# Earlier loads of the cached keys and values, and a ring of three for the negated row minima, in the attention stage of a decoder layer

## The chip, the cores and the metric

The kernel runs on one core of a Trainium2 chip. The metric is the device time of one execution in microseconds. The engines are TensorE (matmuls), VectorE, ScalarE, GpSimd and SyncE; all but TensorE and VectorE issue DMAs here, and in the stage of this change all DMAs are issued by SyncE. In the profile they stand as PE (PEld for its weight loads), DVE, ACT, POOL and SP (SPq for what its queue issues).

## The reference

One layer of a decoder is computed for a prompt of 2048 tokens and for 8 samples of 4 new tokens each, whose past keys and values lie in a cache. The layer has a projection, a recurrent head group, dilated sliding-window attention, an output projection and a mixture of experts. The attention is what matters here:

```
DILATED_CONFIGS = ((128, 1), (512, 4), (2048, 16))      # window, dilation; 8 heads of 64

def _strided_band_attn(q, k, v, window, dilation):      # prompt: blocks of 128 rows of one residue
    ...
    sc = jnp.einsum('bnqhd,bnkhd->bnhqk', qb, kw).astype(jnp.float32) * dh ** -0.5
    sc = jnp.where(mask[None, :, None], sc, NEG_INF)
    m = jnp.max(sc, axis=-1, keepdims=True)
    p = jnp.exp(sc - m)
    l = jnp.sum(p, axis=-1, keepdims=True)
    o = jnp.einsum('bnhqk,bnkhd->bnqhd', (p / l).astype(v.dtype), vw)
    ...

def _dilated_attn_sample(q, k, v, k_buf, v_buf):        # samples: 129 keys per dilation, from the cache
    ...
        sc = jnp.einsum('bthd,btjhd->bthj', q, kg).astype(jnp.float32) * dh ** -0.5
        lse = jax.nn.logsumexp(sc, axis=-1)
        p = jnp.exp(sc - lse[..., None])
        outs.append(jnp.einsum('bthj,btjhd->bthd', p.astype(v.dtype), vg))
    ...
```

The results of the three dilations are merged with weights from their maxima and denominators; the kernel does that in a later stage, which reads what this stage stored.

## The kernel before, in words

The layer is a sequence of stages with a barrier between them. The change is in `attention` (from line 1224).

**Prompt.** There are 48 blocks of 128 query rows: 16 for each dilation. Each is worked in two halves of four heads, so there are 96 units u = 2n and 2n + 1. The first block of each residue has 128 keys, all others 256; the sixteen blocks of dilation 16 (n = 32 to 47) are all first blocks. Keys and queries lie in SBUF, transposed; the keys are turned block by block at the start (`turn_x`, line 1445). In round u of its loop TensorE computes the scores of unit u + 2 (line 1463), turns the probabilities of u (`turn_p`, line 1483), multiplies those of u - 1 with the values (`weigh`, lines 1497 and 1498), and in odd rounds does a piece of a sample's work. VectorE in round u first does the mask and the row minima of unit u + 2 (`mask_min`, line 1615; the queries carry the sign and the scale, so that the minimum of the negated score plays the part of the maximum), then copies half of the turned probabilities (`p_copy`, line 1623), then does a piece of a sample's work. ScalarE takes the exponentials of u + 1 (line 1565) with the minima as bias, copies the other half, and copies the result of u - 1 to the tile `O`, a ring of NO = 3 (line 1579), for which it waits until the stores of block n - 3 have landed.

**Minima.** They are written to `NM`, one tile for all 48 blocks, and nobody waits to write there. The result tile and the minima of block n are stored by `store(n)` (lines 1306 and 1307), both counted by the semaphore `o_st[n % NO]`.

**Samples.** Sample b has a place in the loop, `at(b) = 13 + 8 * b`. Its cached keys come in three groups (256 KiB, 1 MiB and 1 MiB, for dilations 1, 4 and 16), its cached values likewise, its query as a broadcast to all partitions (1 MiB), and its new value rows as 8 KiB. GpSimd multiplies keys by query (`product`, line 1414); the product of the third group, and so on, waits for VectorE's sum of the product two before it, as these are double buffered. VectorE sums (line 1646) in rounds at(b) - 6, - 5 and - 3; in round at(b) the scores are turned and their maxima taken, in round at(b) + 4 the probabilities are turned back, GpSimd spreads them by key tile (line 1422), and in round at(b) + 6 TensorE multiplies them by the cached values in 18 matmuls (`weigh_sample`, line 1518).

**The queue.** SyncE issues every DMA of this stage in one order, written out by hand. In iteration n it issues the key block n + 3 (line 1290, while there are any), the prompt values of block n + 2 (line 1300), then what the samples need (lines 1311, 1317, 1329, 1335 and 1336), and last the store of block n - 1, before which it waits until both halves of that block have been copied. So it enters iteration n once block n - 2 is stored. Each load of a buffer still in use waits first, in the queue's order: `load_sample_k(b, g)` for the product of sample b - 1 and group g, `load_sample_v(b, g)` for the last matmul of sample b - 1, `store_sample(b)` for its result.

By iteration, the samples' DMAs were placed like this, with b counted so that all are for sample b:

| DMA | before | after |
|---|---|---|
| keys, first group | 1 + 4b | 4b - 1 |
| query, keys second group | 2 + 4b | 4b - 1 |
| keys, third group | 3 + 4b | 4b + 1 |
| values, first and second group | 8 + 4b | 7 + 4b |
| values, third group, and new value rows | 9 + 4b | 7 + 4b |
| stores of its result (six) | 12 + 4b | 11 + 4b |

Sample 0 is loaded at n = 0 to 4 in both, and its keys and values are left out of the table; in the kernel before the stores of sample 7 stand at n = 40, in the kernel after at n = 39.

## Time and profile before

| | |
|---|---|
| median of 3 runs | 3607.88 us (3606.35 to 3614.04) |
| the profiled execution | 3606.35 us |
| its span, first to last instruction | 3604.6 us |
| TensorE matmul, share of the span | 88% |
| VectorE, ScalarE, GpSimd | 37%, 28%, 9% |
| HBM read and written | 409.18 MB and 148.50 MB |
| attention stage | about 1612 to 2067 us |
| its work on VectorE at the mask, line 1615 | 384 instructions, 117.3 us |

The span is what the profiler saw from the first instruction to the last; the execution's own time has 1.8 us more around it. A matmul's busy time overlaps the next one's. In rows of a timeline the columns are start, duration, engine, line, operation, output and input tile, and in brackets the idle time of the engine before it with what ended it. In rows of stretches they are the stretch and its length, then busy time and instructions of each engine, the granted TensorE clock (1.00 is 2.4 GHz, 0.50 is 1.2 GHz), the share of time in which the 16 DMA engines were busy, and GB/s.

### The profile page before, as it was taken

To read this page: it belongs to the slowest core of one execution; us is meant where nothing else is said; L and a number is where in the kernel's file an instruction comes from. 1 tells how busy PE (TensorE), PEld (TensorE's weight loads), DVE (VectorE), ACT (ScalarE), POOL (GpSimd) and SP (SyncE) were. 2 spreads that over 40 slices of the span, in tenths; PEclk is the share of its full clock that TensorE was granted. 3 is DMA by queue.
4 is the path that set the end of the run, shared out by engine and by line. 5 is a ranking of instruction groups with operands and counts; after the bars stand their busy time and mean duration, and the time that the engine had idled before them with its cause. 6 is when DMAs were issued, how large, how long until landed. Compare 5 with 4: busy or idle time off the path is not lost. (4 is left out here: it accounts for less than half of the span.)

```text
span 3604.6 us, 75447 instructions
## 1 busy us (share of the span) xinstructions
PE 3171.0 (88%) x31053; PEld 2166.8 (60%) x31054; DVE 1331.3 (37%) x3298; ACT 1013.7 (28%) x2152; POOL 319.3 (9%) x343
## 2 busy tenths in 40 slices
PE   6999999999879888969999859986999999999920
PEld 4667766667668888867776725543555555555500
DVE  3445544444134333426655346643111111111135
ACT  4334443333222222216444523320111111111112
POOL 0000000000010000003432000000001110111011
PEclk9999999999679999989999979987999999999965
DMA  6111111111542323328555465515778776676755
GB/s 216 49 66 65 65 49 60 55 51 56 66 169 109 110 101 115 120 91 266 185 177 154 105 224 177 168 59 206 251 244 279 247 275 221 245 278 211 249 195 204
DMA packets 302886, 561.48 MB, mean 156 GB/s; under 512 B 98866, under 2 KB 123186, under 8 KB 295972
## 3 DMA queue, kind: packets, MB, share of 16 engines
q1 hardware_dynamic: 267684, 458.90, 38.1%
q0 software_dynamic: 20784, 73.15, 5.5%
q10 hardware_dynamic: 14160, 25.70, 2.1%
q8 instruction: 198, 3.24, 0.4%
q14 instruction: 60, 0.49, 0.0%
HBM read 409.18 MB, written 148.50 MB: 155 GB/s over the span
## 5 line engine op out<-in xcount | busy, mean ns | idle before, releaser
L294 PE MATMUL proj_main_ps<-proj_xt,proj_w 128*128 128x257 f32 (+1 forms) x1728 | 391.4, 382 | 0.0
L294 PEld LDWEIGHTS proj_main_ps<-proj_xt,proj_w 128*128 128x128 f32 x1728 | 329.5, 204 | 40.9
L2409 PE MATMUL moe_gate<-moe_w,moe_xt 128*64 128x256 f32 x2624 | 299.7, 382 | 6.6 <-DMA moe_w<-in_expert_w_dram 5.9
L2425 PE MATMUL moe_y_ps<-moe_w,moe_ht 128*64 128x512 f32 x1312 | 301.2, 601 | 3.1 <-ACT moe_ht L2464 3.1
L2409 PE MATMUL moe_up<-moe_w,moe_xt 128*64 128x256 f32 x2624 | 301.3, 383 | 0.0
L2409 PEld LDWEIGHTS moe_gate<-moe_w,moe_xt 128*64 128x64 f32 x2624 | 189.6, 138 | 136.9 <-issue 47.8
L317 PE MATMUL proj_main_ps<-proj_w,proj_xt 128*128 128x512 f32 (+1 forms) x560 | 249.1, 599 | 0.0
L2162 PE MATMUL out_proj_ps<-out_w,out_ct 128*128 128x512 f32 x544 | 240.6, 596 | 0.0
L2409 PEld LDWEIGHTS moe_up<-moe_w,moe_xt 128*64 128x64 f32 x2624 | 180.3, 137 | 97.4 <-issue 13.6
L2475 ACT ACTIVATE moe_sg<-moe_gate 128x256 f32<-128x256 f32 x82 | 31.4, 383 | 542.0 <-PE moe_gate L2409 542.0
L2425 PEld LDWEIGHTS moe_y_ps<-moe_w,moe_ht 128*64 128x64 f32 x1312 | 87.3, 137 | 158.6 <-issue 155.2
L1148 DVE COPY_PREDICATED rwkv_t<-rwkv_cons,rwkv_level_ps 128x512 f32<-128x512 uint32 (+1 forms) x168 | 109.3, 660 | 188.8 <-PE rwkv_level_ps L866 188.7
L317 PEld LDWEIGHTS proj_main_ps<-proj_w,proj_xt 128*128 128x128 f32 (+1 forms) x560 | 103.1, 185 | 124.5 <-issue 123.0
L2511 DVE COPY moe_y<-moe_y_ps 128x512 f32<-128x512 f32 x82 | 56.7, 692 | 313.6 <-PE moe_y_ps L2425 313.6
L2162 PEld LDWEIGHTS out_proj_ps<-out_w,out_ct 128*128 128x128 f32 x544 | 101.7, 192 | 115.1 <-issue 115.1
L1615 DVE CUSTOM_DVE_ANT_0 att_sc<-att_s_ps,att_mask 128x256 f32<-128x256 f32 (+1 forms) x384 | 117.3, 361 | 106.0 <-PE att_s_ps L1463 105.9
L866 PE MATMUL rwkv_level_ps<-rwkv_t,rwkv_w 64*64 64x64 f32 x2688 | 152.5, 222 | 3.4 <-issue 3.4
L2460 ACT COPY moe_xt<-moe_xt_ps 128x512 f32<-128x512 f32 x83 | 48.6, 585 | 353.7 <-PE moe_xt_ps L2402 353.7
L1565 ACT ACTIVATE att_sc<-att_sc,att_nm 128x256 f32<-128x256 f32 (+1 forms) x384 | 145.5, 453 | 0.0
L2517 DVE TENSOR_TENSOR moe_hd<-moe_sg,moe_gate 128x256 f32<-128x256 f32 x82 | 34.6, 421 | 286.4 <-ACT moe_sg L2475 286.4
L1463 PE MATMUL att_s_ps<-att_kt,att_qt 64*128 64x256 f32 (+1 forms) x768 | 139.3, 490 | 0.9 <-DVE att_pt L1623 0.5
L866 PEld LDWEIGHTS rwkv_level_ps<-rwkv_t,rwkv_w 64*64 64x64 f32 x2688 | 135.2, 138 | 4.9 <-issue 4.9
(336 smaller groups left out, 5093.7 us busy)
## 6 DMA issues: line engine op xcount, KB each, us to landing
moe_w<-in_expert_w_dram SPq DMA_DIRECT2D x96, 2048.0 KB, 10.3
y_rows<-rwkv_zero POOLq DMA_DIRECT2D x65, 512.0 KB, 4.8
y_rows<-moe_y ACTq DMA_DIRECT2D x164, 128.0 KB, 6.2
ft_p<-proj_uf SPq DMA_DIRECT2D x32, 642.0 KB, 3.4
rwkv_feat<-ft_p SPq DMA_DIRECT2D x16, 1284.0 KB, 7.2
att_s_k<-in_cache_att_k_dram SPq DMA_DIRECT2D x16, 1024.0 KB, 8.1
att_s_v<-in_cache_att_v_dram SPq DMA_DIRECT2D x16, 1024.0 KB
o_p<-att_o SPq DMA_DIRECT2D x48, 260.0 KB, 2.1
```

Of the source, the lines that this page charges most:

```text
L294: last = mm(out[:, 0:w + 1], W[:, k, kind * C + m * P:kind * C + (m + 1) * P], XT[n % 2][:, k, 0:w + 1], start=(k == 0), stop=(k == KT - 1))
L317: last = mm(o, x, W[:, k, j * C:(j + 1) * C], start=(k == 0), stop=(k == KT - 1))
L866: last = mm(level_ps[g][part(c), hh * P + DH:(hh + 1) * P], W[g][part(c), hh, :], T[i % 3][part(c), h, DH:P], start=True, stop=True, skip_ ...
L1148: v.copy_predicated(T[i % 3][:, 4 * g:4 * g + 4, k0:P], wide(level(l)[:, k0:P], 4).bitcast(U32), four(level_ps[g][:])[:, :, k0:P]).then_in ...
L1463: last = mm(s_ps[u % 2][e][:, pl * 2 * P + k_from(u):(pl + 1) * 2 * P], QT[rows, q, q_at:q_at + d * (P - 1) + 1:d], KT[rows, q, k_at:k_at ...
L1565: nc.scalar.activation(SC[u % NSC][:, hl, k0:], SC[u % NSC][:, hl, k0:], ACT.Exp, bias=NM[:, n, 4 * half + hl:4 * half + hl + 1], scale=-1 ...
L1615: v.tensor_tensor_reduce(SC[u % NSC][:, hl, k0:], s_ps[u % 2][e][:, pl * 2 * P + k0:(pl + 1) * 2 * P], mask[:, k0:], 1.0, 3e38, ALU.add, A ...
L2162: last = mm(proj_ps[j][:], CT[t % 2][:, k, :], W[:, k, 512 * j:512 * (j + 1)], start=(k == 0), stop=(k == KT - 1))
L2409: last = mm(bank[j * HB:(j + 1) * HB, 0:HF], XT[:, q, r * HB:(r + 1) * HB], W[:, k, j * HF:(j + 1) * HF], start=(k == 0), stop=(k == KT - ...
L2425: last = mm(py[j * HB:(j + 1) * HB, :], HT[:, c, r * HB:(r + 1) * HB], W2[s][:, k, j * 512:(j + 1) * 512], start=(k == 0), stop=(k == FE / ...
L2460: nc.scalar.copy(XT[:].rearrange("p k t -> p (k t)"), px[:]).then_inc(xt_ready, 1)
L2511: v.tensor_copy(Y[:], py[:]).then_inc(y_ev, 1)
```

## The change

The minima go into a ring of three small tiles instead of one large one. Because a tile is used again three blocks later, VectorE waits, ahead of the first half of block n, until the stores of block n - 3 have landed. The samples' values are loaded in one place instead of two; keys, queries, values and the samples' stores are issued in earlier iterations of SyncE's loop, as the table above shows. Of the loads of sample b + 1 the query and the first two groups of keys now stand in iteration 3 + 4b, which is also the iteration in which the values of sample b - 1 and the stores of sample b - 2 stand.

```diff
--- before.py
+++ after.py
@@ -1244,7 +1244,7 @@
         V = ring("v", [P, H, VW], NV)
         SC = ring("sc", [P, 4, 2 * P], NSC)
         PT = ring("pt", [P, 4, 2, P], 2)
-        NM = sb("nm", [P, NBK, H])
+        NM = ring("nm", [P, H], NO)
         O = ring("o", [P, H, VW], NO)
         s_ps = [[ps(f"s_ps{k}_{e}") for e in range(2)] for k in range(2)]
         t_ps = [ps(f"t_ps{j}") for j in range(2)]
@@ -1304,7 +1304,7 @@
                 sp.wait_ge(o_copied, 2 * n + 2)
                 dst = lambda x: x[c].rearrange("(i d) k -> d i k", d=d)[r, b * P:(b + 1) * P, :]
                 sp.dma_start(dst(o_out), O[n % NO][:].rearrange("p h k -> p (h k)")).then_inc(o_st[n % NO], 16)
-                sp.dma_start(dst(m_out), NM[:, n, :]).then_inc(o_st[n % NO], 16)
+                sp.dma_start(dst(m_out), NM[n % NO][:]).then_inc(o_st[n % NO], 16)
 
             def load_sample_q(b):
                 rows = qkv_s[b * T:(b + 1) * T, 0:C]
@@ -1321,12 +1321,12 @@
                     sp.wait_ge(s_prod, 3 * (b - 1) + g + 1)
                 cached(SK, cache_k, b, g, sk_ld[g])
 
-            def load_sample_v(b, g):
+            def load_sample_v(b):
                 if b >= 1:
                     sp.wait_ge(s_weighted, b)
-                cached(SV, cache_v, b, g, sv_ld)
-                if g == 2:
-                    sp.dma_start(VN[:], qkv_s[b * T:(b + 1) * T, 2 * C:3 * C]).then_inc(sv_ld, 16)
+                for g in range(3):
+                    cached(SV, cache_v, b, g, sv_ld)
+                sp.dma_start(VN[:], qkv_s[b * T:(b + 1) * T, 2 * C:3 * C]).then_inc(sv_ld, 16)
 
             def store_sample(b):
                 sp.wait_ge(s_o, b + 1)
@@ -1362,28 +1362,20 @@
                 if 1 <= n < 3:
                     load_sample_k(0, n)
                 if n == 4:
-                    for g in range(3):
-                        load_sample_v(0, g)
-                for b in range(B + 1):
-                    slot = n - (at(b) - 7) // 2
-                    if slot == 1 and b >= 2:
-                        load_sample_v(b - 1, 0)
-                        load_sample_v(b - 1, 1)
-                        store_sample(b - 2)
-                    if slot == 2 and b >= 2:
-                        load_sample_v(b - 1, 2)
-                    if b + 1 < B:
-                        if slot == 2:
-                            load_sample_k(b + 1, 0)
-                        if slot == 3:
-                            if b >= 1:
-                                sp.wait_ge(s_prod, 3 * b)
-                            load_sample_q(b + 1)
-                            load_sample_k(b + 1, 1)
-                        if slot == 4:
-                            load_sample_k(b + 1, 2)
-                if n == (at(B - 1) + 11) // 2:
-                    store_sample(B - 1)
+                    load_sample_v(0)
+                for b in range(B):
+                    if n == (at(b) - 7) // 2 and b + 1 < B:
+                        if b >= 1:
+                            sp.wait_ge(s_prod, 3 * b)
+                        load_sample_q(b + 1)
+                        load_sample_k(b + 1, 0)
+                        load_sample_k(b + 1, 1)
+                    if n == (at(b) - 3) // 2 and b + 1 < B:
+                        load_sample_k(b + 1, 2)
+                    if n == (at(b) + 9) // 2:
+                        if b + 1 < B:
+                            load_sample_v(b + 1)
+                        store_sample(b)
                 if n >= 1:
                     store(n - 1)
             store(NBK - 1)
@@ -1562,7 +1554,7 @@
                 k0 = k_from(u)
                 for hl in range(4):
                     a.wait_ge(masked, 4 * u + hl + 1)
-                    nc.scalar.activation(SC[u % NSC][:, hl, k0:], SC[u % NSC][:, hl, k0:], ACT.Exp, bias=NM[:, n, 4 * half + hl:4 * half + hl + 1], scale=-1.0).then_inc(exped, 1)
+                    nc.scalar.activation(SC[u % NSC][:, hl, k0:], SC[u % NSC][:, hl, k0:], ACT.Exp, bias=NM[n % NO][:, 4 * half + hl:4 * half + hl + 1], scale=-1.0).then_inc(exped, 1)
 
             def p_copy(u):
                 a.wait_ge(p_turned, u + 1)
@@ -1610,10 +1602,12 @@
                 v.wait_ge(scored, u + 1)
                 if u >= NSC:
                     v.wait_ge(p_turned, u - NSC + 1)
+                if n >= NO and half == 0:
+                    v.wait_ge(o_st[n % NO], 32 * (n // NO))
                 for hl in range(4):
                     pl, e = hl // 2, hl % 2
                     v.tensor_tensor_reduce(SC[u % NSC][:, hl, k0:], s_ps[u % 2][e][:, pl * 2 * P + k0:(pl + 1) * 2 * P], mask[:, k0:], 1.0, 3e38,
-                                           ALU.add, ALU.min, NM[:, n, 4 * half + hl:4 * half + hl + 1]).then_inc(masked, 1)
+                                           ALU.add, ALU.min, NM[n % NO][:, 4 * half + hl:4 * half + hl + 1]).then_inc(masked, 1)
 
             def p_copy(u):
                 v.wait_ge(p_turned, u + 1)
```

## Rows read from the trace of the kernel before

**Rows 1.** The page: the engines over the whole span.

```profile
PE 3171.0 (88%) x31053; PEld 2166.8 (60%) x31054; DVE 1331.3 (37%) x3298; ACT 1013.7 (28%) x2152; POOL 319.3 (9%) x343
```

**Rows 2.** Busy time by stretch, attention stage.

```profile
1700.00:1750.00 50.00, 49.94 (x357) 38.24 (x356) 33.37 (x101) 28.52 (x68) 16.50 (x5) 1.00 0.67 198
```

**Rows 3.** Waits, attention stage: who for whom, total us, times, longest.

```profile
DVE att_sc L1615 <- PE att_s_ps L1463: 105.9, 71, 17.9
...
PE att_t_ps L1518 <- issue: 8.8, 2, 4.6
```

**Rows 4.** Timeline of TensorE: the value products of samples 1, 6 and 7.

```profile
1747.96 7.92 PE L1518 MATMUL att_t_ps<-att_s_v,att_s_lm 128*96 128x512 f32 x18
...
1967.12 9.76 PE L1518 MATMUL att_t_ps<-att_s_v,att_s_lm 128*96 128x512 f32 x18 [4.20 <-issue]
...
2003.86 10.16 PE L1518 MATMUL att_t_ps<-att_s_v,att_s_lm 128*96 128x512 f32 x18 [4.60 <-issue]
```

**Rows 5.** Timeline of SyncE's queue at the last samples, and two stretches.

```profile
1956.63 0.59 SPq L1317 DMA_DIRECT2D att_s_v<-in_cache_att_v_dram  x1
...
1957.00:1961.00 4.00, 4.00 (x32) 3.47 (x33) 2.76 (x13) 2.54 (x9) 2.27 (x2) 1.00 0.46 34
1961.00:1967.00 6.00, 1.93 (x18) 1.58 (x16) 2.61 (x10) 2.85 (x10) 0.00 (x0) 0.75 0.96 283
```

**Rows 6.** Timeline of SyncE's queue, iterations 11, 15 and 19.

```profile
1719.51 0.32 SPq L1306 DMA_DIRECT2D o_p<-att_o  x1
...
1720.35 1.14 SPq L1290 DMA_DIRECT2D att_x<-out_dram  x1
...
1727.95 0.33 SPq L1306 DMA_DIRECT2D o_p<-att_o  x1
...
1761.16 0.33 SPq L1306 DMA_DIRECT2D o_p<-att_o  x1
...
1805.85 0.33 SPq L1306 DMA_DIRECT2D o_p<-att_o  x1
```

**Rows 7.** Timeline of VectorE and TensorE, masks of blocks 13, 17, 21.

```profile
1733.25 0.41 DVE L1615 CUSTOM_DVE_ANT_0 att_sc<-att_s_ps,att_mask 128x256 f32<-128x256 f32 x1
...
1735.44 0.61 PE L1445 MATMUL att_t_ps<-att_ident,att_x 128*128 128x128 f32 x4
...
1774.80 0.42 DVE L1615 CUSTOM_DVE_ANT_0 att_sc<-att_s_ps,att_mask 128x256 f32<-128x256 f32 x1 [0.98 <-PE att_s_ps L1463]
...
1779.24 0.42 DVE L1615 CUSTOM_DVE_ANT_0 att_sc<-att_s_ps,att_mask 128x256 f32<-128x256 f32 x1 [0.45 <-PE att_s_ps L1463]
...
1781.10 0.30 PE L1511 MATMUL att_t_ps<-att_ident,att_s_p 96*128 96x96 f32 x1 [0.47 <-DVE att_pt L1623]
...
1820.55 0.42 DVE L1615 CUSTOM_DVE_ANT_0 att_sc<-att_s_ps,att_mask 128x256 f32<-128x256 f32 x1 [0.98 <-PE att_s_ps L1463]
```

**Rows 8.** By line: key load 1639.2, minima's store 1644.3, all their stores.

```profile
L1317 SPq DMA_DIRECT2D att_s_k<-in_cache_att_k_dram x1: 1902/1902/1902, 1639.2 to 1639.2; - x1
...
DMA to landing us min/median/max: 10.1/10.1/10.1
...
L1307 SPq DMA_DIRECT2D m_p<-att_nm x1: 433/433/433, 1644.3 to 1644.3; - x1
...
DMA to landing us min/median/max: 5.8/5.8/5.8
...
DMA to landing us min/median/max: 1.9/1.9/6.3
```

**Rows 9.** SyncE's queue (packets, MB, share), 1719 to 1762; one stretch.

```profile
q1 hardware_dynamic: 7289, 8.46, 65.1%
...
1658.00:1666.00 8.00, 7.38 (x65) 6.57 (x63) 6.91 (x20) 4.31 (x10) 4.54 (x1) 1.00 1.04 376
```

**Rows 10.** Timeline of GpSimd.

```profile
1649.44 4.54 POOL L1414 TENSOR_TENSOR att_s_prd<-att_s_k,att_s_q 128x2048 f32<-128x2048 f32 x1 [10.53 <-DVE att_s_sn L1630]
...
1752.74 9.01 POOL L1414 TENSOR_TENSOR att_s_prd<-att_s_k,att_s_q 128x2048 f32<-128x2048 f32 x2 [10.15 <-DMA att_s_q<-qkv_s]
```

## The prediction

> **What bounds the kernel now.** I read the page first for the share of each engine [rows 1], then TensorE's stretches in the attention stage, the only stage that the change touches [rows 2]. The stage runs from about 1612 to 2067 us, a little over an eighth of the span. From 1700 to 1750 us TensorE is busy 49.94 of 50 us, so a microsecond that TensorE loses there is a microsecond of the kernel. I then read the waits of the stage [rows 3]. No row there makes TensorE, VectorE or ScalarE wait for a load of cached keys. VectorE's waits at the mask (line 1615) are waits for TensorE, 105.9 us in 71 pieces: it has slack on average, and the question is how much of it lies at the places where the change adds a wait. Two waits are not slack. The product of probabilities and cached values (line 1518) is preceded by 8.8 us of idle TensorE in two pieces.
>
> The timeline shows them [rows 4]: before the seventh and the eighth sample TensorE idles 4.20 and 4.60 us, and its 18 matmuls then take 9.76 and 10.16 us where an undisturbed sample's take 7.92 us. The queue explains it [rows 5]: the last 1 MiB of the seventh sample's values is issued at 1956.63, moves only from about 1961 us on (34 GB/s from 1957 to 1961, 283 GB/s from 1961 to 1967), and TensorE starts at 1967.12. The granted clock was 0.75 on average from 1961 to 1967, so in part of it the level of 1.2 GHz, and TensorE had just gone idle.
>
> **Earlier values: a gain.** Values move from iterations n = 8 and 9 + 4b of SyncE's loop to 7 + 4b, for all but the first sample. For the eighth sample that is two iterations of some 6 us before the old last part. Both stalls should go: 4.20 + 4.60 + (9.76 - 7.92) + (10.16 - 7.92) = 12.9 us. From below the gain is nothing, if the stall has another cause. No other sample waits (two pieces in all), so earlier values are worth nothing there.
>
> **Where the loads now meet.** In the new loop, iterations n = 11, 15, 19, 23 and 27 issue, all ahead of the store of block n - 1: a prompt value block (256 KiB), all values of a sample (2.25 MiB), its new value rows, six small stores of the previous sample, a query broadcast (1 MiB) and two groups of keys (1.25 MiB). With the 260 KiB store behind them this is 5.26 MB, where one iteration had 2.25 MiB at most in steady state. SyncE alone needs about 8 us to issue it (16 DMAs, and those in rows 6 take 0.3 to 1.1 us each), as much as a block lasts (1719.5 to 1728.0).
>
> **The new wait.** The mask minima go into a ring of three, so the mask of block m + 3 (VectorE) now waits for the stores of block m. Call T the time at which block n - 2 is stored. The store of block n - 1 comes about 8 to 9 us after T, and the mask that needs its landing started at 1733.25 for n = 11, which is T + 13.7, and at 1774.80 for n = 15, T + 13.6 [rows 6, 7]. For n = 19 (T = 1805.85) it started at 1820.55, T + 14.7; I use that for 23 and 27. The store leaves at 1727.95 for n = 11 and such a store lands 1.9 us after its issue in the median [rows 8], so in the old rhythm it is there some 3 us ahead, and the wait alone costs nothing: what covers it is TensorE's own unit of work between the two.
>
> Behind the burst it doesn't. A store issued at 1644.30 while a 1 MiB key load from 1639.2 was still on its way (it took 10.1 us, to 1649.3) took 5.8 us, to 1650.1 [rows 8]. I read this as one queue served in order. The first load leaves at T + 0.85 (1720.35 - 1719.51). The rate: over a period of four blocks the queue moved 8.46 MB in 65.1% of 43 us, 302 GB/s while it moved, and the best long stretch has 376 GB/s [rows 9]. I take 320, nearer to the first, which has the same mix of transfers. So 5.26 MB take 16.4 us; with the 1.9 us that a small store takes alone the store lands at T + 0.85 + 16.4 + 1.9 = T + 19.2. For n = 11, with one more 256 KiB block of keys ahead, it lands at 1720.35 + 17.3 + 1.9 = 1739.5.
>
> How much lateness VectorE can take is in rows 7. At n = 11 the copy behind the mask ends just where TensorE turns the next key block (1735.44), so none. At n = 15 it works on from the first mask to the second with 0.45 us of idle ahead of that (1779.24), and TensorE already waits 0.47 us for the copy after it (1781.10): 0.45 us can be absorbed. The next ones have the same pattern. Stalls of TensorE: n = 11: 1739.5 - 1733.25 = 6.3; n = 15: 19.2 - 13.6 - 0.45 = 5.1; n = 19, 23, 27: 19.2 - 14.7 - 0.45 = 4.05 each, 12.15. Sum 23.5 us. Lower bound with 376 GB/s: 3.7 + 2.65 + 3 x 1.6 = 11 us. Upper bound with 302 GB/s and the 3.5 us in which the queue moved nearly nothing after the last part of the values was issued [rows 5]: 10.8 + 9.6 + 3 x 8.5 = 46 us.
>
> The Trainium skill (DMA: Bandwidth & Descriptors, section Where 436 GB/s comes from) puts the limit of one core's HBM traffic at about 358 GB/s; the trace has 376 over 8 us, so the measurement decides. By an estimate from that page the five stalls would add up to about 15 us instead of 23.5.
>
> **Clock.** An idle of 4.20 us cost another 1.84 us through matmuls at half clock [rows 4]. The five stalls are of that length, so 5 x 1.84 = 9.2 us; from below nothing, if shorter gaps leave the clock alone, and 5 x 2.24 = 11 us from above.
>
> **Start.** At n = 3 the second sample's second key group waits for the product of the first sample's second group, which ends at 1649.44 + 4.54 = 1654.0 [rows 10], and store 2 stands behind it, then the values of the first sample at n = 4. Queries and keys of 1.25 MiB also enter a queue that at 1649.3 had only just landed the key load before them and still held the last 1 MiB of the prompt's queries [rows 8]. From 1649.3 some 3.6 MB at 320 GB/s put the landing near 1661, while store 2 is due 8.4 us after the one of 1644.3 and its landing needed 5.3 us later (1733.25 - 1727.95), at 1658. I take 3.5 us, between 1 and 10. **Tail.** At n = 35 values, prompt values and six small stores (2.89 MB) precede store 34: it lands at T + 11.8, needed at about T + 9 because these blocks last 5.2 us, with about 1 us of slack: 1.5 us, between 0 and 5. At n = 7 (2.75 MiB of loads) and 31 the store lands within a microsecond of its need: 0.
>
> **Costed at nothing.** The ring's smaller tile and its other addresses. ScalarE's wait for the same store comes later than VectorE's and is met. The old loads' removal from n = 5 to 9: nobody waited. GpSimd's products move earlier (in rows 10 they wait 10.15 us for a query), with VectorE's sums where they were. SyncE's waits on products in steady state: even at their old place the products ended at 1752.74 + 9.01 = 1761.75, before SyncE asks, after 1762 [rows 6, 10].
>
> **Sum.** 23.5 + 9.2 + 3.5 + 1.5 - 12.9 = +24.8 us. The profiled execution took 3606.35 us (span 3604.6, 1.8 us around it), so 3631.2; the median of the runs is 1.5 us above it: 3632.7, and I say 3633.
>
> **Rivals.** *Stalls gone, none new (faster).* The store isn't held up, or VectorE's slack covers it, and only the 12.9 us are seen: 3595. For it: the old queue was drained when a store came, and VectorE idles 106 us at this line. Against it: it needs 5.26 MB within 11 us, 480 GB/s, or a store that overtakes, which rows 8 contradict. It decides if the store lands before T + 13.7. Chance 0.13.
>
> *Even.* The queue runs at its best rate and the gaps are too short for the clock: 11 + 1 - 12.9 = about 0, 3607. Chance 0.13 for all within 0.2% (7.2 us, about what a measurement of this kernel can tell).
>
> *SyncE held at a product.* The third load of the burst waits for GpSimd; if products ended 3 us later than before, each of five bursts would grow by 3 us: 3648. Against it: their queries now come earlier. Chance 0.04.
>
> *Values are not why TensorE idles.* Then 12.9 us stay lost: 3646. Against it: the stretches of rows 5, where data move until TensorE starts. Counted with the next case. *Queue much slower.* All upper bounds: 46 + 11 + 10 + 5 - 12.9 = +59, 3667. Together 0.06. My forecast, slower by 8 to 54 us, has 0.64.
>
> **Range.** The low end is the even case with part of the faster one, 3603, and the high end 3662; beyond lie 0.12 and 0.06. Slower by over 0.2%: 0.64 + 0.04 + 0.06 = 0.74.
>
> **What the profile after would show.** VectorE's idle before line 1615 released by a store of the minima, in about five pieces of 4 to 6 us plus a few short ones. Landings of the two block stores near 10 us at n = 11 to 27, and SyncE issue times of several us at the query or key loads. TensorE idle in the same places, with clock 0.5 behind. No idle before line 1518 at the seventh and eighth samples. It is wrong if the stores land in 2 us behind the loads, if the burst drains at over 450 GB/s, or if VectorE had more slack than I read.

## The result, and the profile after

The kernel after takes 3694.68 us (median of 4 runs, 3690.24 to 3702.20), the kernel before, run beside it, 3610.96 us. The ratio is 1.0232, with a 95% interval of 1.0207 to 1.0259: slower by 84 us. The prediction had the sign, and 25 us. The profiled execution took 3683.05 us with a span of 3681.3, 76.7 us more than the one of before. Between these two executions the rest of the program, which the change leaves as it was, took 9.6 us less (7.6 ahead of the attention stage, 2.0 behind it), and the stage itself 86.3 us more. The stretches of the stage, from its first matmul to its last, in the kernel before and in the kernel after:

```profile
1616.05:2066.02 449.97, 431.36 (x2817) 327.61 (x2817) 252.17 (x963) 230.62 (x608) 129.41 (x33) 0.97 0.59 181
```

```profile
1608.48:2144.79 536.31, 478.84 (x2817) 371.03 (x2817) 249.87 (x963) 231.95 (x608) 129.26 (x33) 0.82 0.52 151
```

With the same 2817 matmuls TensorE is idle for 38.9 us more (57.5 against 18.6) and busy for 47.5 us more, at a granted clock of 0.82 on average instead of 0.97. All sums below are made against these 86.3.

The waits of the attention stage in the kernel after (who for whom, total us, times, longest), which answer to [rows 3]:

```profile
DVE att_sc L1609 <- DMA m_p<-att_nm: 68.0, 11, 11.6
...
ACT att_sc L1557 <- DVE att_nm L1609: 28.1, 8, 7.0
PE att_t_ps L1475 <- DVE att_pt L1617: 19.4, 4, 6.8
```

The first row is new: VectorE, at the mask, waits eleven times for a store of the minima. The others are its followers: ScalarE's exponentials wait for the minima, TensorE for VectorE's copies. The row of 8.8 us of idle before the value product, the second of [rows 3], has no successor: these waits are gone.

TensorE's timeline shows where this costs time (start, duration, instruction, idle before it and what ended it). These are six of the fourteen gaps over 1 us behind the start of the stage; together the fourteen make 51.1 us.

```profile
1658.91 1.09 PE L1437 MATMUL att_t_ps<-att_ident,att_x 128*128 128x128 f32 x4 [4.96 <-issue]
...
1748.55 1.09 PE L1437 MATMUL att_t_ps<-att_ident,att_x 128*128 128x128 f32 x4 [11.45 <-issue]
1801.25 1.09 PE L1475 MATMUL att_t_ps<-att_ident,att_sc 128*128 128x128 f32 x4 [6.82 <-DVE att_pt L1617]
...
2014.25 0.30 PE L1503 MATMUL att_t_ps<-att_ident,att_s_p 96*128 96x96 f32 x1 [1.81 <-DVE att_pt L1617]
2053.68 1.09 PE L1475 MATMUL att_t_ps<-att_ident,att_sc 128*128 128x128 f32 x4 [6.25 <-ACT att_sc L1557]
2090.28 0.63 PE L1475 MATMUL att_t_ps<-att_ident,att_sc 128*128 128x128 f32 x4 [1.64 <-ACT att_sc L1557]
```

The burst of iteration n = 11 in SyncE's queue, the same iteration as the first two rows of [rows 6]: block 9 is stored at T = 1721.00, and the minima's store of block 10 is issued behind all loads of the burst.

```profile
1721.00 0.32 SPq L1306 DMA_DIRECT2D o_p<-att_o  x1
...
1729.91 1.02 SPq L1317 DMA_DIRECT2D att_s_k<-in_cache_att_k_dram  x2
1730.97 0.48 SPq L1306 DMA_DIRECT2D o_p<-att_o  x1
1731.51 0.49 SPq L1307 DMA_DIRECT2D m_p<-att_nm  x1
```

By line, that store of the minima, and below it the same for one store in the last blocks:

```profile
L1307 SPq DMA_DIRECT2D m_p<-att_nm x1: 491/491/491, 1731.5 to 1731.5; - x1
...
DMA to landing us min/median/max: 14.7/14.7/14.7
...
L1307 SPq DMA_DIRECT2D m_p<-att_nm x1: 433/433/433, 2083.1 to 2083.1; - x1
...
DMA to landing us min/median/max: 5.6/5.6/5.6
```

And VectorE's masks that waited, in bursts 11 and 15, and in the last blocks:

```profile
1746.37 0.43 DVE L1609 CUSTOM_DVE_ANT_0 att_sc<-att_s_ps,att_mask 128x256 f32<-128x256 f32 x1 [11.55 <-DMA m_p<-att_nm]
...
1799.30 0.42 DVE L1609 CUSTOM_DVE_ANT_0 att_sc<-att_s_ps,att_mask 128x256 f32<-128x256 f32 x1 [10.25 <-DMA m_p<-att_nm]
...
2052.26 0.29 DVE L1609 CUSTOM_DVE_ANT_0 att_sc<-att_s_ps,att_mask 128x128 f32<-128x128 f32 x1 [8.70 <-DMA m_p<-att_nm]
2088.86 0.29 DVE L1609 CUSTOM_DVE_ANT_0 att_sc<-att_s_ps,att_mask 128x128 f32<-128x128 f32 x1 [4.08 <-DMA m_p<-att_nm]
```

SyncE issues the burst in about 10 us and is held by nothing in it (the longest issue takes 1.60 us); the queue does the rest. The store issued at 1731.51 lands 14.7 us later, at 1746.2, and the mask starts at once: at T + 25.4, where before it started at T + 13.7 [rows 7]. In the next two bursts (T = 1776.39 and 1830.79) the mask starts at T + 22.9 and T + 22.0.

The last reading is of the clock (stretch, then busy time and instructions by engine, the granted clock, the DMA share, GB/s):

```profile
1740.00:1750.00 10.00, 1.46 (x6) 1.16 (x8) 3.63 (x10) 0.33 (x1) 0.00 (x0) 0.50 1.01 336
1750.00:1760.00 10.00, 10.00 (x75) 8.42 (x75) 6.83 (x22) 5.81 (x14) 4.21 (x2) 0.85 0.04 16
...
2090.00:2100.00 10.00, 9.72 (x54) 8.95 (x54) 4.08 (x28) 4.69 (x15) 0.00 (x0) 0.55 0.31 81
...
2130.00:2140.00 10.00, 10.00 (x54) 9.32 (x53) 3.14 (x19) 5.63 (x18) 0.00 (x0) 0.50 0.08 29
```

In the middle the 10 us behind the longest gap average 0.85. In the last blocks, after a gap of 1.64 us, it is at 0.50 until the stage ends, although TensorE is counted busy for 10.00 of 10 us. But the clock also falls where no gap stands ahead. Call a sample's value product (18 matmuls of 512 columns) dense, and the blocks' own matmuls, of 64 to 256 columns, light. At 1879.3, 1933.9 and 1988.6 the clock falls about 3 us behind the end of a dense product, with TensorE busy throughout, and the first time it is back at 1889.6, in the middle of light blocks:

```profile
1880.00:1889.00 9.00, 9.00 (x43) 7.93 (x41) 3.57 (x17) 2.87 (x7) 0.00 (x0) 0.50 0.29 79
1890.00:1900.00 10.00, 10.00 (x77) 9.07 (x78) 6.07 (x23) 6.07 (x18) 0.00 (x0) 1.00 1.06 301
```

What the lower clock costs in the last blocks is seen in the timeline: one unit of those blocks in the kernel after,

```profile
2103.74 1.24 PE L1455 MATMUL att_s_ps<-att_kt,att_qt 64*128 64x128 f32 x8
2104.91 1.11 PE L1475 MATMUL att_t_ps<-att_ident,att_sc 128*128 128x128 f32 x4
2105.82 1.80 PE L1490 MATMUL att_o_ps<-att_v,att_pt 128*128 128x65 f32 x8
2107.55 1.24 PE L1455 MATMUL att_s_ps<-att_kt,att_qt 64*128 64x128 f32 x8
```

and one at a granted clock of 1.00, in the run e13 told below, which has the same queue:

```profile
2067.88 1.23 PE L1455 MATMUL att_s_ps<-att_kt,att_qt 64*128 64x128 f32 x8
2069.04 0.66 PE L1475 MATMUL att_t_ps<-att_ident,att_sc 128*128 128x128 f32 x4
2069.53 1.00 PE L1490 MATMUL att_o_ps<-att_v,att_pt 128*128 128x65 f32 x8
2070.48 1.23 PE L1455 MATMUL att_s_ps<-att_kt,att_qt 64*128 64x128 f32 x8
```

A unit lasts 3.81 us (1.24 to 1.24) instead of 2.60. From 2090.9 to the last product, which ends at 2144.8, are 14.1 such units: 14.1 x 1.21 = 17 us.

**The ledger of the 86.3 us.** Idle that is new: 51.1 us, of it 35.3 in the five bursts, 6.1 at the start, 1.8 at n = 31 and 7.9 in the last blocks. Idle that is gone: 8.8 before the value products and 3.5 in small pieces and in the stage's first microseconds. Together that is 38.9, up to rounding. The 47.5 us in which TensorE is busy for longer with the same matmuls I put down to the lower clock: 17 of it in the last blocks by the rows above, and some 30 elsewhere, net of what the two old gaps had cost. These 30 are a difference and are not split further; part of them is in the three stretches (24 us in all) that no gap precedes.

### The profile page after: what moved, and what is told of

Its sections match the earlier page's. It is cut to its first block and busy times, and to the rows that moved or that the text cites. A ratio compares the mean times of both kernels' runs of the same rounds, so it can differ in the third digit from the quotient of the medians.

```text
span 3681.3 us, 75447 instructions
## 1 busy us (share of the span) xinstructions
PE 3211.8 (87%) x31053; PEld 2202.3 (60%) x31054; DVE 1328.4 (36%) x3298; ACT 1014.6 (28%) x2152; POOL 319.6 (9%) x343
## 5 line engine op out<-in xcount | busy, mean ns | idle before, releaser
L1490 PE MATMUL att_o_ps<-att_v,att_pt 128*128 128x65 f32 x768 | 149.4, 314 | 0.0
```

The source lines that it names most:

```text
L1490: last = mm(out, PT[u % 2][:, hl, 1, :], V[n % NV][:, h, :], start=first(u), stop=True, skip_group_check=True)
```

## The experiments

Fourteen kernels ran. Each ratio is to runs of the kernel before beside it, on the same chip (medians 3592.95 for e1 to e4, 3586.83 for e5 to e8, 3592.18 for e9 to e12, 3591.45 for e13 and e14).

**The parts by themselves.** e1 is the kernel before with the ring and the wait alone:

```
-        NM = sb("nm", [P, NBK, H])
+        NM = ring("nm", [P, H], NO)
...
+                if n >= NO and half == 0:
+                    v.wait_ge(o_st[n % NO], 32 * (n // NO))
```

> The kernel before with the ring of three for the minima and its wait, and the old order of SyncE's queue. Theory (the wait costs only where a burst of loads stands ahead of the store): VectorE's waits for a store of the minima come to a few us in all, most of them at the start, and the time is 3611 to 3622 us; a single late landing among the last blocks may add up to 20 us through the clock. Rival (the ring alone is the cost): 3670 us or more, with waits in nearly every period of four blocks.

e2 is the kernel after with one tile of minima and no wait, so the new queue alone:

```
-        NM = ring("nm", [P, H], NO)
+        NM = sb("nm", [P, NBK, H])
...
-                if n >= NO and half == 0:
-                    v.wait_ge(o_st[n % NO], 32 * (n // NO))
```

> The changed kernel with one tile for all minima and no wait on VectorE; its queue as changed. Theory: the stores still land 15 to 25 us late behind the bursts, but nobody needs them then, so the only effect left is the one of the early values, -12.9 us: 3598 us, up to 3608 if ScalarE's wait for the same stores, three rounds later, now binds by a few us. Rival (the loads themselves do the harm, through late prompt values or contention): over 3630 us.

e3 is the kernel before with only the values read together and an iteration earlier:

```
+                    if slot == 0 and b >= 2:
+                        for g in range(3):
+                            load_sample_v(b - 1, g)
                     if slot == 1 and b >= 2:
-                        load_sample_v(b - 1, 0)
-                        load_sample_v(b - 1, 1)
...
-                        load_sample_v(b - 1, 2)
```

> The kernel before with one tile for all minima, and of the change only this: the values of samples 1 to 7 issued together in iteration 7 + 4b. Theory: TensorE no longer idles before the value products of the seventh and eighth samples (4.2 and 4.6 us) and its clock doesn't fall there: 3598 us, between 3594 and 3604. Rival (the stall there has another cause): 3611 us.

e4 is the kernel after with a ring of six, so that a block waits for stores six blocks back:

```
-        NM = ring("nm", [P, H], NO)
+        NM = ring("nm", [P, H], 2 * NO)
...
+                if n >= 2 * NO and half == 0:
+                    v.wait_ge(o_st[n % NO], 32 * (n // NO - 1))
```

> The changed kernel with a ring of six tiles for the minima, so that VectorE waits for the stores of block n - 6, some 25 us further back. Theory (the depth of the ring is what fails against bursts of about 20 us): no wait for a store of the minima over 1 us, and the time of the kernel with one tile and the new queue, 3598 to 3608 us. Rival (the wait itself, as an instruction, costs): between 3620 and 3690 us.

Measured: e1 3611.96 us, ratio 1.0056 (1.0038 to 1.0074); e2 3589.58 us, 0.9985 (0.9970 to 1.0000); e3 3594.53 us, 0.9999 (0.9978 to 1.0020); e4 3587.33 us, 0.9991 (0.9972 to 1.0010). The ring alone costs 20 us, the queue alone costs nothing, and both together 84: most of the loss comes only with both. With a ring of six VectorE waits for no store, and the loss is gone. The wait of e1 is short in the middle, where the old queue holds no burst, but it is not free. The row of its waits, and its longest, in VectorE's timeline:

```profile
DVE att_sc L1617 <- DMA m_p<-att_nm: 23.9, 8, 6.8
```

```profile
1995.24 0.29 DVE L1617 CUSTOM_DVE_ANT_0 att_sc<-att_s_ps,att_mask 128x128 f32<-128x128 f32 x1 [6.76 <-DMA m_p<-att_nm]
```

Five of its eight waits are in the last blocks, which last 5.2 us each. (This profile is of the fastest of its six runs, so it shows less than the 20 us.) The prediction had costed the wait alone at nothing. In e3 the idle before the value products is gone and the time is not: the stretch

```profile
2020.00:2060.00 40.00, 40.00 (x212) 36.36 (x210) 14.90 (x99) 20.33 (x64) 0.00 (x0) 0.50 0.24 68
```

of its profiled execution shows the last blocks at the lower clock with no gap of TensorE ahead of them: it fell at 1996.0, 3 us behind the eighth sample's dense product, and stayed for 68 us. So these blocks can lose their clock without the wait too, in some executions. The same happens in the middle: in e4, where VectorE waits for no store, light blocks run for 34 us at half clock behind a dense product, and in e2 for 28 us, until the next one.

```profile
1790.00:1824.00 34.00, 34.00 (x158) 29.99 (x157) 14.86 (x53) 12.24 (x32) 4.56 (x1) 0.50 0.62 182
```

**What makes the store late.** e5 puts keys and queries back where they were, so that a burst is split:

```
-                        load_sample_q(b + 1)
-                        load_sample_k(b + 1, 0)
-                        load_sample_k(b + 1, 1)
...
+                        if slot == 2:
+                            load_sample_k(b + 1, 0)
+                        if slot == 3:
...
+                            load_sample_q(b + 1)
+                            load_sample_k(b + 1, 1)
```

> The changed kernel with the ring of three and its wait, and with the values and the result stores where the change put them, but with queries and keys at the places of the kernel before. The burst ahead of store n - 1 falls from 5.26 MB to about 3.9 MB where the third key group stands in it too, and the query is gone. Theory (the landing is late by what stands ahead of it): the waits at n = 11 to 27 shrink by about 5 us each, from 7 to 11.5 us to 2 to 6 us, and the time is 3615 to 3640 us against 3593 of before on that chip. Rival (any burst of values holds the store as long, because of a pause in the queue and not of bytes): over 3655 us.

e6 lets ScalarE's queue issue the blocks' stores, behind its second copy of the result, in place of SyncE's:

```
+                if half == 1:
...
+                    a.dma_start(dst(o_out), O[n % NO][:].rearrange("p h k -> p (h k)")).then_inc(o_st[n % NO], 16)
+                    a.dma_start(dst(m_out), NM[n % NO][:]).then_inc(o_st[n % NO], 16)
```

> The changed kernel with the two stores of each block issued by ScalarE after its copy, so that they don't stand behind the loads in SyncE's queue; loads and ring as changed. Theory (one queue served in order holds the stores): they land in 2 to 5 us even beside a burst, VectorE waits for minima's stores under 10 us in all instead of 68, and the time is 3595 to 3615 us, with some us for 0.8 us of issue per block on ScalarE. Rival (the memory or the DMA engines themselves are full, whatever the queue): waits of over 5 us in each burst and over 3640 us.

e7 moves the six small stores of a sample's result behind the block's stores:

```
-                        store_sample(b)
                 if n >= 1:
                     store(n - 1)
+                for b in range(B):
+                    if n == (at(b) + 9) // 2:
+                        store_sample(b)
```

> The changed kernel with only the six small result stores of a sample moved behind the block's stores in the same iteration. They are 25 KB in rows of 4 and 260 bytes. If they cause the pause of about 4 us that the queue shows inside each burst, the waits of VectorE shrink by 3 to 4 us each, and the time by 20 to 30 us, to 3645 to 3655 us where the changed kernel would take about 3677 on that chip. If the bytes ahead are what counts, the waits stay as they are and the time within 10 us of the changed kernel's.

Measured: e5 3640.33 us, 1.0157 (1.0130 to 1.0184), waits 41.2 us in 9; e6 3666.12 us, 1.0215 (1.0188 to 1.0241); e7 3673.91 us, 1.0242 (1.0215 to 1.0269), waits 57.5 us in 10. Splitting the burst takes a third of the loss away: the waits in the five bursts fall to 2.6 to 6.1 us, as expected, but 56 us over the kernel before beside it is more than the theory's 22 to 47; a wait of 8.4 us stays among the last blocks. In e7 the time is after's, as expected if the bytes ahead are what counts; what it says of the small stores is told below. e6 is the miss that teaches most. Its minima's store in the burst of n = 11, issued at 1730.70, lands in two thirds of the time. Its waits:

```profile
DVE att_sc L1612 <- DMA m_p<-att_nm: 64.5, 17, 7.1
```

That store by line:

```profile
L1574 ACTq DMA_DIRECT2D m_p<-att_nm x1: 472/472/472, 1730.7 to 1730.7; - x1
...
DMA to landing us min/median/max: 9.4/9.4/9.4
```

The long waits shrink to 4.4 to 7.1 us, but seventeen waits add up to as much as eleven did, so "one queue served in order" was only part of the reason: a 4 KB store takes 9.4 us beside 5 MB of loads from another queue as well, where only the 260 KB store of the same block stands ahead of it. The Trainium skill (DMA: Bandwidth & Descriptors, section Issuing engines are not separate DMA queues) says that DMAs of all issuers run on the same 16 engines and interleave; the run agrees, with these 9.4 us. Another issuer shares the delay out instead of removing it.

**What the rate in a burst is.** In each burst the queue has a weak stretch of about 4 us (1735 to 1739 in the first, at T + 14):

```profile
1735.00:1737.00 2.00, 2.00 (x20) 1.95 (x18) 0.00 (x0) 0.87 (x2) 2.00 (x1) 1.00 0.91 156
1737.00:1739.00 2.00, 0.09 (x1) 0.00 (x0) 0.00 (x0) 0.38 (x1) 2.00 (x1) 1.00 0.83 90
...
1741.00:1743.00 2.00, 0.00 (x0) 0.00 (x0) 0.00 (x0) 0.00 (x0) 0.00 (x0) 0.50 0.98 395
```

The DMA engines are counted busy at 0.83 to 0.91 in it and move 90 to 156 GB/s. e10 takes a suspect out, the 8 KB load of the new value rows:

```
-                sp.dma_start(VN[:], qkv_s[b * T:(b + 1) * T, 2 * C:3 * C]).then_inc(sv_ld, 16)
+                if b == 0:
+                    sp.dma_start(VN[:], qkv_s[b * T:(b + 1) * T, 2 * C:3 * C]).then_inc(sv_ld, 16)
...
-                pe.wait_ge(sv_ld, 64 * b + 64)
+                pe.wait_ge(sv_ld, 48 * b + 64)
```

> The kernel after, without the 8 KB transfer of the new value rows of samples 1 to 7 (they use sample 0's, so that part of the computation is left out). Theory (this small transfer is what makes the weak stretch of about 4 us in each burst): the waits for the minima's buffer in blocks 11, 15, 19, 23 and 27 shrink by 3 to 4 us each, the time falls by 10 to 20 us. Rival (the weak stretch belongs to the large transfers themselves, or to their order): waits and time as after, within 5 us.

Measured: 3670.58 us, 1.0224 (1.0180 to 1.0268), waits 58.4 us in 9, longest 10.4. That is after's loss: the rival. So it isn't the value rows. The six small stores are not cleared by e7. There they are issued 4 us later, counted from T, land within 13 us of their issue, and the weak stretch comes later too, at T + 20 to T + 26 (T = 1718.59), still ahead of the landing of block 10's minima at T + 23.6:

```profile
1739.00:1741.00 2.00, 0.00 (x0) 0.00 (x0) 0.00 (x0) 0.00 (x0) 0.00 (x0) 0.50 1.22 130
1741.00:1743.00 2.00, 0.00 (x0) 0.00 (x0) 0.59 (x3) 0.00 (x0) 0.00 (x0) 0.50 0.94 134
```

The last blocks say the same. In the kernel after the six small stores of sample 7, at n = 39, stand right ahead of block 38's, which lands after 5.6 us, and block 41 waits. In e7 they stand one store further back: block 39's then takes 6.1 us, and the wait is at block 42. In e1 they are at n = 40, again ahead of block 39's, which takes 5.1 us, and again block 42 waits. The wait moves with them, so they make that one. For the weak stretch it is only where it lies that points to them; no run leaves them out of a burst, so its cause is not shown.

**What a gap costs, and where.** e8 and e9 hold VectorE up by the same work in the kernel before, in round 78 (last blocks) and in round 24 (middle):

```
+            def hold():
+                for j in range(4):
+                    v.wait_ge(q_ld[j], 16)
+                for j in range(2):
+                    v.tensor_reduce(IDLE[:, j * 8:(j + 1) * 8], QT[:, j, :].rearrange("p (h k) -> p h k", h=8), AX.X, ALU.add)
...
+                if u == 78:
+                    hold()
```

> The kernel before with one added delay of about 4.4 us on VectorE (two sums over 2048 columns of the queries, results unused) ahead of the mask in round 78, among the last blocks. Theory (a gap there takes the clock of TensorE to its lower level, and nothing in this light work brings it back before the stage ends): 2 to 3 us of idle, then granted clock 0.50 until the end of the stage, blocks of 7.64 instead of 5.19 us, in all 15 to 25 us more than before. Rival (the clock comes back after some us, as it did in the middle of the stage before): 4 to 6 us more.

> The kernel before, with VectorE held up by some 4.4 us once more, now in round 24, in the middle of the kernel, where a sample's dense attention product follows within 25 us (the earlier hold was in the last blocks). The work that holds it is two added sums, whose results nothing uses. Theory (a gap costs its own idle, and the clock is given back soon where dense work follows; in the last blocks it isn't): TensorE idle 2 to 4.5 us, 1 to 3 us more at the lower clock, 4 to 7 us in all, against 25 us for the same hold in the last blocks. Rival (a gap costs the same anywhere, the 25 us came from something else in the added sums): 20 us or more here too. Second rival (TensorE's queue of work covers it): under 2 us.

Measured: e8 3615.47 us, 1.0071 (1.0045 to 1.0097); e9 3596.09 us, 1.0019 (0.9997 to 1.0042). The same hold costs 25 us (16 to 35) in the last blocks and 7 (-1 to 15) in the middle, although TensorE's gap is the shorter one there. e8's gap, 1.83 us, in TensorE's timeline, and the stretches behind it:

```profile
2023.12 0.69 PE L1484 MATMUL att_t_ps<-att_ident,att_sc 128*128 128x128 f32 x4 [1.83 <-ACT att_sc L1566]
```

```profile
2020.00:2030.00 10.00, 8.17 (x49) 7.40 (x48) 5.59 (x28) 4.67 (x15) 0.00 (x0) 0.68 0.21 56
2030.00:2040.00 10.00, 10.00 (x54) 9.09 (x53) 4.07 (x27) 5.04 (x16) 0.00 (x0) 0.50 0.33 93
```

The stretches of e9, with its gap of 4.19 us in the first of them (the last row begins within the second):

```profile
1720.00:1730.00 10.00, 5.81 (x42) 4.88 (x43) 10.00 (x13) 3.38 (x8) 4.52 (x1) 0.80 0.62 196
1730.00:1740.00 10.00, 10.00 (x76) 8.46 (x74) 6.88 (x22) 5.87 (x15) 2.02 (x1) 0.86 0.39 142
1733.00:1743.00 10.00, 10.00 (x88) 8.91 (x87) 7.48 (x24) 6.20 (x14) 2.02 (x1) 1.00 0.30 90
```

In e9 the two averages below 1.00 are the time of 6.8 us at half clock (10 x 0.20 / 0.5 + 10 x 0.14 / 0.5); 2.4 us of it lie in the gap itself, the other 4.4 lose up to 2.2 us, and 4.19 + 2.2 = 6.4 us is near the 7 measured. The clock is back from 1733 on, 10 us ahead of the next dense product. In e8 the clock stays at 0.50 in every later stretch and doesn't come back before the stage ends.

**Each place for itself.** e13 is after with a wait for the block four before from block 32 on, three before up to there; e14 is its complement (both with four tiles in memory):

```
+                back = 3 if n < 32 else 4          # e14: n >= 32
+                if n >= back and half == 0:
+                    v.wait_ge(o_st[(n - back) % NO], 32 * ((n - back) // NO + 1))
```

> Blocks 0 to 31 wait for the stores of the block three before, as after; from block 32 on a block waits for the block four before it (a ring of four in memory). Theory (the last blocks cost 6.25 + 1.64 us of idle and some 20 to 25 us at the lower clock, the bursts of blocks 11 to 27 the rest): 48 to 60 us over before, against 83 us for after; the granted clock is 1.00 in the last blocks. Rival (the lower clock in the last blocks comes anyway, as in the run with values together): 70 us or more over before.

> The complement: from block 32 on a block waits for the stores of the block three before, as after; the blocks before wait for the block four before them. Theory: 20 to 35 us over before, and with the loss of its complement it makes up the 83 us of after within 15 us (each place pays for itself). Rival (the waits in the last blocks need the bursts' delays ahead of them): within 8 us of before.

Measured: e13 3640.45 us, 1.0149 (1.0106 to 1.0192), 54 us; e14 3605.57 us, 1.0037 (1.0012 to 1.0063), 13 us. e13 is as expected, and its last blocks run at 1.00. The waits of the last blocks cost time by themselves (the interval of e14 is 4 to 23 us), but less than expected, and the rival's "within 8 us" is not excluded; the two add up to 67 us (roughly 49 to 85 by their intervals) of 84: compatible with a sum, at the edge. The kernel before is not the best base for this sum, as its queue is the old one. e12, told below, has e13's and e14's queue and tiles and waits for the block four before everywhere. Over e12, by the ratios, e13 costs 62 us, e14 22 and the kernel after 92, so 8 us are left between the sum and the whole, and e14's 22 (roughly 10 to 33) is above the rival's 8. e14's ten runs tell why one number describes it badly: they lie between 3591.16 and 3632.11 us. Its profiled execution is the slowest of them, with one long wait of 9.5 us, a gap of 7.02 us behind it, and in the last blocks half the clock to their end:

```profile
1997.93 1.09 PE L1475 MATMUL att_t_ps<-att_ident,att_sc 128*128 128x128 f32 x4 [7.02 <-ACT att_sc L1557]
```

```profile
2080.00:2090.00 10.00, 10.00 (x52) 9.66 (x51) 3.13 (x18) 4.85 (x15) 0.00 (x0) 0.50 0.11 38
```

The 40 us that this execution has over before are not the wait's alone. The eighth sample's dense product brought the clock back at 2010.2; it fell again at 2020.4, 3 us behind that product and with no gap, as in e3, and stayed down to the end. And from 1788 to 1822, where this kernel waits for nothing, it was down for 34 us as in e4. So part of e14's scatter is the clock's, and this trace doesn't tell how much of the cost is the waits' own.

**Two versions meant to gain.** e11 spaces the samples by ten rounds instead of eight, in the kernel before, so that fewer light blocks stand behind the last dense product:

```
-    at_new, first_at, period = 7, 13, 8
+    at_new, first_at, period = 7, 13, 10
```

> The kernel before with a single tile of minima and stores where they were before, a sample's values read together, and a sample every 10 rounds of the projections in place of every 8, so that the last sample's dense attention product comes later and fewer light blocks stand behind it. Theory (light last blocks at the lower clock cost about 20 us where they are behind the last dense product): 10 to 20 us faster than before. Rival (VectorE, not TensorE, bounds the rounds, and the clock in the last blocks is at the higher level in most executions of before): within 5 us of before, or slower by up to 10 us where the sample's work no longer falls beside the blocks that it was spaced for.

e12 is the kernel after with a ring of four:

```
-        NM = ring("nm", [P, H], NO)
+        NM = ring("nm", [P, H], 4)
...
-                if n >= NO and half == 0:
-                    v.wait_ge(o_st[n % NO], 32 * (n // NO))
+                if n >= 4 and half == 0:
+                    v.wait_ge(o_st[(n - 4) % NO], 32 * ((n - 4) // NO + 1))
```

> The kernel after with a ring of four buffers for the minima in place of three, so that a block waits for the stores of the block four before it. Theory (the stores land 22 to 25 us behind the start of a burst, and a block lasts 8.4 us there): the wait of block 11's burst falls from 11.5 to about 3 us, that of 15 from 10.3 to about 1.5 us, the others in bursts to nothing or under 1 us, none in the last blocks; the time is 3 to 15 us over before, so less than a fifth of after's loss is left. Rival (the stores are late by whatever the ring allows, as the queue falls further behind): waits of 5 us or more remain in most bursts, and half of the loss.

Measured: e11 3645.39 us, 1.0135 (1.0100 to 1.0170), outside both expectations. Its profile shows where: it has more light blocks between two samples, and in several such places they run at half clock, with TensorE all but fully busy; two of them:

```profile
2020.00:2050.00 30.00, 29.13 (x153) 26.17 (x151) 16.95 (x77) 14.20 (x45) 13.87 (x4) 0.50 0.68 228
...
2080.00:2100.00 20.00, 20.00 (x106) 18.09 (x106) 7.50 (x48) 10.08 (x32) 2.02 (x1) 0.50 0.61 191
```

e12 takes 3583.88 us, 0.9977 (0.9957 to 0.9996): a little faster than before, and it was expected slower by 3 to 15 us. One tile more, 4 KB, and the waits are

```profile
DVE att_sc L1609 <- DMA m_p<-att_nm: 4.2, 2, 2.2
```

2.17 us in burst 11 (3 were expected) and 2.00 at the first of the last blocks. Its profiled execution shows the gain that was forecast: the stage lasts 438.8 us, 11.2 less than before, and behind the first 15 us of the stage the clock is down for 3.4 us only. It is the best version here: by the ratios it beats the kernel after by 2.5% and the one before by 0.2%. e4, with six tiles, is within 0.2% of both e12 and before.

## Why the prediction was right in kind and wrong in size

**The mechanism: right.** The stores of block n - 1 stand behind 5.26 MB, VectorE waits for them at the mask, and TensorE idles behind VectorE. e1, e2 and e4 show it: neither part has the loss, and a deeper ring ends it. All five bursts of the forecast have their wait and their gap. Three signs that the prediction named came out larger or not at all: the pieces of VectorE's idle are 7.1 to 11.6 us instead of 4 to 6, the landing took 14.7 us instead of near 10, and SyncE's issues are not held. "One queue served in order" was too simple (e6).

**Five bursts: in its bounds.** 35.3 us where the sum has 23.5 (11 to 46). Burst 15 is typical: forecast landing T + 19.2, mask at T + 22.9. With 1.9 us for the store itself and 0.85 us for the start, 5.26 MB took 20.2 us, 261 GB/s instead of 320. The weak stretch of 4 us is about the difference; I had seen one in [rows 5] and left it to the upper bound. The slack of VectorE was read a little too small: in burst 15 the mask came 22.9 - 13.6 = 9.3 us late and TensorE's gaps make 7.9 us, so 1.4 us were absorbed instead of 0.45.

**Start and n = 31: small.** 6.1 us for 3.5 (1 to 10), and 1.8 us for none.

**Last blocks: the first step that failed.** "1.5 us, between 0 and 5" for the tail at n = 35 was 6.25 us: store 34 landed at T + 16.1 instead of T + 11.8 (T = 2036.00), so 2.89 MB went at 217 GB/s, not 320. And "costed at nothing" for the wait alone was another 1.64 us some 35 us later, without any large load: a 4 KB store behind the six small stores that took 5.6 us instead of 1.9 was enough, because blocks of 5.2 us leave a ring of three about 1 us. I had used the short blocks for n = 35 only; that the wait alone costs nothing I had read from the lead of "some 3 us" in the middle, where blocks last 8.4 us. The row with a maximum of 6.3 us was on view [rows 8]: such landings occur.

**Clock: the step that failed most.** "5 x 1.84 = 9.2 us", net of the two old gaps' 4.1 us a plus of 5.1, stands against 47.5. Of these 17 are in the last blocks and some 30 elsewhere, where there are more and longer gaps than five (one of them 11.45 us) and three stretches at half clock that no gap precedes. The price of 1.84 us a gap was taken from gaps in front of 18 dense matmuls, and was used as if it held anywhere. In e8 a gap of 1.83 us cost 25 us, and in e9 one of 4.19 us cost 7. So what a gap costs depends on where it lies. TensorE's busy share doesn't tell: it is 10.00 of 10 us in blocks that stay at 0.50. The Trainium skill (TensorE: Matmul & The Clock Gate, section What's actually happening) says that the clock follows how busy the array has been of late; by the profile's count of busy time the trace doesn't agree in these blocks, where TensorE is counted busy throughout. In light blocks of 256 keys the clock came back by itself (kernel after, 1889.6; e9, 1732.8; e4, after 34 us); in those of 128 keys it came back only with the next dense product or, in e3 and e7, some 2 us before the stage's end.

**Gain: mis-sized in time.** The 8.8 us of idle went, as forecast, but the time of 12.9 us did not come: e3 measures 0 (within 0.2%) and e2 5 us (0 to 11). In their profiled executions the clock takes back what was saved: e2, e3 and e4 run for 31, 68 and 34 us at half clock with no gap ahead, and only e12's, which doesn't, has a stage that is 11.2 us shorter than before. How often this happens, I can't say from one profile each.

**Rivals and range.** "Queue much slower", with all upper bounds, came nearest (3667), and held less than it should: the measured time lies beyond the range because two upper bounds were too low, 5 us for the tail and above all 11 for the clock.

The terms side by side, in us of the attention stage in the profiled executions:

| term | forecast (bounds) | measured |
|---|---|---|
| idle in five bursts | 23.5 (11 to 46) | 35.3 |
| idle at the start | 3.5 (1 to 10) | 6.1 |
| idle at n = 31 | 0 | 1.8 |
| idle in the last blocks | 1.5 (0 to 5) | 7.9 |
| old idle gone | - 8.8 | - 8.8 |
| small pieces of idle, and the stage's first microseconds | 0 | - 3.5 |
| clock, net of the old gaps | 9.2 - 4.1 = 5.1 | 47.5 |
| sum | 24.8 | 86.3 |

The whole span grew by 76.7 us, as the rest of the program took 9.6 us less.

**Left open:** what makes the weak stretch in a burst; what decides where, and in which executions, light blocks lose their clock without a gap; and the difference between the sum of e13 and e14 and the whole (17 us over the kernel before, 8 over e12), which is within their scatter but not shown to be only that.

## What to carry to other kernels

When a buffer is made a ring, compare the slack it leaves (depth times the shortest block, less the way to the landing) with the longest landing in the trace, not the median, and do it for each kind of block: here one tile of 4 KB more was worth 2.5%. Moving loads earlier is free only as long as nobody waits for what stands behind them in the queue, or beside them on the DMA engines. Price an idle of TensorE by where it lies: in front of dense matmuls it cost itself and some 2 us here, among the light last blocks the lower clock to the end of the stage. And read the clock of the whole stage, not only behind the gaps: here it also fell without one.

## What was not expected of the hardware

- A light stretch can hold TensorE at 1.2 GHz while it is counted busy: 54 us in the kernel after, 68 us in e3, 34 us in the middle in e4, and in e11 between the samples too. In e3 and e4 no gap stands ahead; the clock fell 3 to 4 us behind a dense product. A unit takes 3.81 instead of 2.60 us; the score product of 64 rows is as long at either level (1.24 and 1.23 us), the others take 1.7 to 1.8 times as long.
- A 4 KB store beside a burst took 9.4 us from another issuer's queue, and 14.7 us behind it in the same queue; one behind six small stores, with no large load ahead, took 5.6 us.
- 16 DMA engines counted busy for 0.83 to 0.91 of a stretch moved 90 to 156 GB/s, against 395 GB/s at 0.98 a few microseconds later.
